# Loading expert weights 1 MB at a time, with neighbouring rows of K in one partition

## What is computed

```python
D_MODEL = 2048; SEQ = 512; N_EXPERTS = 16; TOP_K = 2; D_EXPERT = 512; MOE_BLOCK = 128

def moe_ffn(h, w_router, router_bias, w1, w3, w2):
    ...
    order = jnp.argsort(flat_e)
    ...
    xb = h[buf_tok].reshape(n_blocks, MOE_BLOCK, D)

    def expert_block(args):
        xblk, e = args
        return (jax.nn.silu(xblk @ w1[e]) * (xblk @ w3[e])) @ w2[e]
    ...
    return jnp.zeros_like(h).at[stok].add(yb[dest] * sgate[:, None].astype(h.dtype))
```

## Time and profile before

| what | value |
|---|---|
| time, median of 3 runs | 2569.21 us (2564.76 to 2570.18) |
| profiled execution: its span, first to last instruction | 2558.9 us |
| median less this span | 10.3 us |
| PE busy / VectorE (DVE) / ScalarE (ACT) / GpSimd (POOL) | 89% / 62% / 37% / 24% of the span |
| share of PE in the chain that ended last | 74% |
| DMA | 532 MB, 208 GB/s in the mean; 366 to 392 GB/s in the expert stage |
| granted clock of PE, mean | 0.951 |

### The profile page before, as it was taken

The page is one execution under the profiler, slowest core; times in us unless marked ns, Lnnn a source line. Parts: engine busy times, 40 slices in busy tenths (PEclk is TensorE's granted clock), DMA queues, the critical chain, the costliest instruction groups (busy, mean ns, idle before and its releaser), DMA issues.

```text
span 2558.9 us, 35674 instructions
## 1 busy us (share of the span) xinstructions
PE 2279.9 (89%) x11413; PEld 1875.1 (73%) x11413; DVE 1582.4 (62%) x1942; ACT 947.6 (37%) x1130; POOL 607.5 (24%) x698
## 2 busy tenths in 40 slices
PE   2579999999999999799999998998579999999990
PEld 1179888888888888477777876777557777777770
DVE  2177545555556554566666664523579999999984
ACT  3044322222122212322222222222158777777771
POOL 0035414424443443211111110100201221221222
PEclk9889999999999999799999999999589999999995
DMA  9945422222222222377777775632479999999985
GB/s 375 410 130 164 134 83 77 66 84 68 78 72 76 73 79 74 107 224 226 219 229 234 230 220 198 219 116 70 164 250 368 382 375 390 366 373 392 372 340 214
DMA packets 386604, 532.12 MB, mean 208 GB/s; under 512 B 15072, under 2 KB 261344, under 8 KB 379008
## 3 DMA queue, kind: packets, MB, share of 16 engines
q1 hardware_dynamic: 353216, 392.93, 44.7%
q0 software_dynamic: 33344, 138.63, 15.5%
HBM read 494.77 MB, written 36.73 MB: 208 GB/s over the span
## 4 chain that ended last, share of the span: by engine, by line
PE 74%; DVE 6%; issue 3%; ACT 2%; DMA 2%; POOL 1%; ACTq 0%; SPq 0%; POOLq 0%; DVEq 0%
PE ps L614 11%; PE ps L616 11%; PE ps L615 11%; PE ps L894 6%; PE ps L896 5%; PE ps L895 5%; PE ps L676 4%; DVE e_lo L1776 2%; PE ps L801 2%; PE ps L844 2%; PE ps L802 2%; PE ps L845 2%; PE ps L846 2%; PE ps L803 2%; PE ps L916 1%
## 5 line engine op out<-in xcount | busy, mean ns | idle before, releaser
L1349 DVE TENSOR_TENSOR w_lo<-raw,w_hi 128x1024 fp32r<-128x1024 f32 x272 | 345.0, 1270 | 339.8 <-ACT w_hi L1012 338.6
L1012 ACT CAST w_hi<-raw 128x1024 fp32r<-128x1024 f32 x272 | 285.0, 1049 | 690.4 <-PE ps L616 368.5
L1776 DVE TENSOR_TENSOR e_lo<-e_raw,e_hi 128x1024 fp32r<-128x1024 f32 x384 | 501.8, 1329 | 59.7 <-ACT e_hi L1220 47.8
L614 PE MATMUL ps<-hl_hi,w_hi 128*128 128x512 f32 x1280 | 510.7, 399 | 0.5 <-DVE s_ctx L1422 0.5
L616 PE MATMUL ps<-hl_hi,w_lo 128*128 128x512 f32 x1280 | 499.9, 391 | 0.0
L615 PE MATMUL ps<-hl_lo,w_hi 128*128 128x512 f32 x1280 | 499.1, 390 | 0.0
L1220 ACT CAST e_hi<-e_raw 128x1024 fp32r<-128x1024 f32 x384 | 401.0, 1059 | 162.9 <-PE ps L896 117.5
L616 PEld LDWEIGHTS ps<-hl_hi,w_lo 128*128 128x128 f32 x1280 | 240.8, 188 | 51.6
L614 PEld LDWEIGHTS ps<-hl_hi,w_hi 128*128 128x128 f32 x1280 | 241.2, 188 | 49.3 <-issue 1.7
L615 PEld LDWEIGHTS ps<-hl_lo,w_hi 128*128 128x128 f32 x1280 | 241.3, 189 | 49.1 <-issue 1.7
L894 PE MATMUL ps<-e_hi,xe_hi 128*128 128x512 f32 x512 | 206.6, 404 | 36.1 <-DVE e_lo L1776 33.2
(11 more groups left out here) (331 smaller groups left out, 3681.1 us busy)
## 6 DMA issues: line engine op xcount, KB each, us to landing
e_raw<-in_w_e SPq DMA_DIRECT2D x384, 512.0 KB, 6.9
raw<-in_w_in SPq DMA_DIRECT2D x208, 512.0 KB, 3.7
ada<-in_w_ada POOLq DMA_DIRECT2D x64, 1024.0 KB, 6.0
ada_ring<-in_w_ada SPq DMA_DIRECT2D x16, 2048.0 KB, 17.1
raw<-in_w_out SPq DMA_DIRECT2D x32, 512.0 KB, 4.0
block_outputs<-y_sb POOLq DMA_DIRECT2D x32, 512.0 KB
raw<-in_w_branch_pool SPq DMA_DIRECT2D x16, 512.0 KB, 3.9
raw<-in_w_branch_hgrn SPq DMA_DIRECT2D x16, 512.0 KB, 3.9
```

Source lines behind the costliest of these rows:

```text
L614: mm(dst, hi, rhs_hi[:, k, :], start=(k == 0), stop=False)
L1012: act_e.copy(w_hi[:, hslot, :], raw[:, slot, :]).then_inc(hi_done, 1)
L1349: tt(w_lo[:, hslot, :], raw[:, slot, :], w_hi[:, hslot, :].bitcast(F32), ALU.subtract).then_inc(split_done, 1)
L1776: tt(e_lo[:, hslot, :], e_raw[:, slot, :], e_hi[:, hslot, :].bitcast(F32), ALU.subtract).then_inc(e_split, 1)
```

## The change

The three expert weights are viewed with `(p k)` for `(k p)`: row d = 16 p + k of w_e1 and w_e3 lies in partition p, and row d = 4 p + k of w_e2. A load now takes four neighbouring rows of w_e1 or w_e3, or one whole row of w_e2, for each partition: 2048 numbers, 8 KB in one run, 1 MB in all. It fills two neighbouring slots of `e_raw`; the ring has four such pairs, each with one semaphore. SP waits until both units of the pair that was there are split. There are 12 loads an expert for 24. Casts, splits and matmuls stay at units of 512 KB. So that the tokens agree with the new order of rows, a transpose of `xe` reads every 16th column, one of `act` every 4th.

```diff
--- before.py
+++ after.py
@@ -138,9 +138,9 @@
     w_bh_d = w_branch_hgrn[0].rearrange("(k p) n -> p k n", p=P)
     w_out_d = w_out[0].rearrange("(k p) n -> p k n", p=P)
     w_pg_d = w_pool_group[0].rearrange("g (k p) n -> p g k n", p=P)
-    w_e1_d = w_e1[0].rearrange("e (k p) n -> e p k n", p=P)
-    w_e3_d = w_e3[0].rearrange("e (k p) n -> e p k n", p=P)
-    w_e2_d = w_e2[0].rearrange("e (k p) n -> e p k n", p=P)
+    w_e1_d = w_e1[0].rearrange("e (p k) n -> e p k n", p=P)
+    w_e3_d = w_e3[0].rearrange("e (p k) n -> e p k n", p=P)
+    w_e2_d = w_e2[0].rearrange("e (p k) n -> e p k n", p=P)
     w_r_d = w_router.rearrange("(k p) n -> p k n", p=P)
 
     mod_d = nc.dram_tensor("mod_rows", [1, 4 * D], F32).ap()
@@ -390,7 +390,7 @@
         score_rdy, sel_rdy, pos_mm, onehot_rdy, tab_mm, table_rdy = (sem(s) for s in (
             "score_rdy", "sel_rdy", "pos_mm", "onehot_rdy", "tab_mm", "table_rdy"))
 
-        e_in = raw_in + [sem("e_in6"), sem("e_in7")]
+        e_in = raw_in[0:4]
         e_hi_done, e_split, e_units = sem("e_hi_done"), sem("e_split"), sem("e_units")
         xe_in, xe_T, xe_hi_rdy, xe_rdy = (sem(s) for s in (
             "xe_in", "xe_T", "xe_hi_rdy", "xe_rdy"))
@@ -421,7 +421,7 @@
             return SLOTS + s + 1
 
 
-        E_BASE = [16 * (U_M // SLOTS + KT + 8)] * 4 + [16 * (U_M // SLOTS + KT)] * 2 + [0] * 2
+        E_BASE = 16 * (U_M // SLOTS + KT + 8)
 
 
         @block.sync
@@ -517,35 +517,30 @@
             sp.wait_ge(h2_rdy, NTOK - 1)
             sp.wait_ge(h2_last, 1)
 
-            def load_e(g, slot, src):
-                sp.wait_ge(e_split, g + 1)
+            def load_e(n, slot, src):
+                sp.wait_ge(e_split, n * 2 + 2)
                 sp.sem_inc(sp_own, 1)
-                sp.dma_start(e_raw[:, slot, :].rearrange("p (k n) -> p k n", k=src.shape[1]), src
+                sp.dma_start(e_raw[:, 2 * slot:2 * slot + 2, :].rearrange("p a b -> p (a b)"), src
                              ).then_inc(e_in[slot], 16)
 
-            def w13(w, e, q):
-                return w[ds(e, 1), :, 2 * q:2 * q + 2, :].rearrange("o p k n -> (o p) k n")
-
-            def w2(e, q):
-                return w_e2_d[ds(e, 1), :, q // 2:q // 2 + 1, 1024 * (q % 2):1024 * (q % 2) + 1024
-                              ].rearrange("o p k n -> (o p) k n")
-
-            for q in range(16):
-                load_e(q, q % 8, w13(w_e1_d if q < 8 else w_e3_d, 0, q % 8))
+            def piece(e, n):
+                w, k, rows = (w_e1_d, n, 4) if n < 4 else (w_e3_d, n - 4, 4) if n < 8 else (w_e2_d, n - 8, 1)
+                return w[ds(e, 1), :, rows * k:rows * k + rows, :].rearrange("o p k n -> (o p) (k n)")
+
+            for n in range(8):
+                load_e(n, n % 4, piece(0, n))
             with sp.Fori(1, E) as e:
-                for q in range(24):
-                    src = w13(w_e1_d, e, q) if q < 8 else w13(w_e3_d, e, q - 8) if q < 16 else w2(e - 1, q - 16)
-                    load_e(e * 24 + (q - 8), q % 8, src)
-            for q in range(8):
-                load_e(E * 24 - 8 + q, q, w2(E - 1, q))
+                for n in range(12):
+                    load_e(e * 12 + (n - 4), n % 4, piece(e, n) if n < 8 else piece(e - 1, n))
+            for n in range(8, 12):
+                load_e(E * 12 - 12 + n, n % 4, piece(E - 1, n))
             sp.wait_ge(table_rdy, 1)
             n_extra = sp.value_load(route_i[0:1, 7:8], min_val=0, max_val=NXTRA)
             with sp.Fori(0, NXTRA) as b:
                 with sp.If(b < n_extra):
                     e = sp.value_load(route_i[0:1, ds(b, 1)], min_val=0, max_val=E - 1)
-                    for q in range(24):
-                        src = w13(w_e1_d, e, q) if q < 8 else w13(w_e3_d, e, q - 8) if q < 16 else w2(e, q - 16)
-                        load_e(b * 24 + (E * 24 + q), q % 8, src)
+                    for n in range(12):
+                        load_e(b * 12 + (E * 12 + n), n % 4, piece(e, n))
                 sp.nop()
 
             for i in range(NTOK):
@@ -914,13 +909,14 @@
                 pe.wait_ge(actT_rdy, b + 1)
                 for j in range(4):
                     last = pe.transpose(ps[:, 6 + part % 2, j * P:(j + 1) * P],
-                                        xe[:, (4 * part + j) * P:(4 * part + j + 1) * P], ident[:])
+                                        xe[:].rearrange("t (p k) -> t k p", k=KT)[:, 4 * part + j, :], ident[:])
                 last.then_inc(xe_T, 1)
 
             def turn_act(b):
                 pe.wait_ge(act_rdy, b + 1)
                 for j in range(4):
-                    last = pe.transpose(ps[:, 6, j * P:(j + 1) * P], act[:, j * P:(j + 1) * P], ident[:])
+                    last = pe.transpose(ps[:, 6, j * P:(j + 1) * P],
+                                        act[:].rearrange("t (p k) -> t k p", k=4)[:, j, :], ident[:])
                 last.then_inc(act_T, 1)
 
             def x_ready(b):
@@ -1215,7 +1211,7 @@
 
 
             def e_hi_unit(g, slot, hslot, uses):
-                act_e.wait_ge(e_in[slot], uses + E_BASE[slot])
+                act_e.wait_ge(e_in[slot // 2], uses + E_BASE)
                 act_e.wait_ge(e_units, g + 1)
                 act_e.copy(e_hi[:, hslot, :], e_raw[:, slot, :]).then_inc(e_hi_done, 1)
```

## The result

| | median of the timed runs | ratio to before, 95% interval | span of the profiled execution |
|---|---|---|---|
| before | 2569.69 us (4 runs, 2564.76 to 2571.45) | | 2558.9 us |
| after | 2600.85 us (4 runs, 2592.35 to 2605.99) | 1.0122 [1.0094, 1.015] | 2600.4 us |

The changed kernel is 31 us slower. Two slow executions further down, one of e8_three_pairs (3802.95 us) and one of the kernel before beside it (3406.05 us), are left out of the medians and ratios.

The account below looks back on a forecast made before the run. PE was taken as the bound, the DMA engines nearly one. Span 2558.9 - 1.4 (waits for xe_lo) + 0 (coarseness, small edits) + 0 (transposes) = 2557.5, with timed runs 10.3 us above: 2567.8 us; range 2560 to 2593.

Parts of the forecast that it names:

- the second rival: Expert stage: the coarse ring of 1 MB loads starves ScalarE's casts, 2575 to 2586 us; chance 0.15.
- the price of coarseness: Expert weight loads: later issue and waiting for all of 1 MB cost 0, up to 2.0 us an expert in the range.
- From issue to landing, "5.7 us" for 1 MB: Expert weight loads: 4.5 us where the queue had just run dry, plus 1.24 for 512 KB more.
- so it holds: Quiet part of a turn: a pair lands 5.7 us after issue, ScalarE needs it after about 6.9, no loss.
- Landed at 2114.4 or somewhat later: Tight place: the pair lands 8.7 us after 2105.7; first cast 0.9 us late, inside PE's 1.25 us of cover.
- Nine of the fourteen experts: Experts without half clock have no spare room; each loses 0.75 us (2575 us) or 2.0 us (2586 us).
- Faster runs: Expert weight loads: runs of 8 KB move 422 GB/s, over 415 when saturated, giving the engines 2.2 us of room per expert.
- What of it reaches the end, 1.4 us at most: Only PE's waits for xe_lo made by DMA can be gained: 1.4 us in the whole run.
- The transposes at 0: Strided weight loads of xe and act stay hidden under the identity's pass, starts 0.11 us apart: cost 0.
- The first rival: Strided weight loads of transposes outrun the identity's pass: 22.4 us slower, 2590.2 us; chance 0.27.
- PE's old waits stay: PE's waits behind act's transposes, 0.31 and 2.06 us an expert, come from POOL's multiply and remain.
- The places at half clock: Expert stage: five stretches partly at 1.2 GHz cost 1.5 us each; missing all five gives 2560 us; chance 0.10.

Follow-up runs that it names:

- e8_three_pairs: The changed kernel with three pairs of slots for four: 2669.70 us, ratio 1.0399 to the kernel before.
- e2: The kernel before with the new order of rows and strided transposes, still 512 KB loads in eight slots, runs of 4 KB: 2573.05 us, ratio 1.0018.
- e9: The kernel before with twelve slots of 512 KB for eight: 2565.02 us, ratio 1.0007.
- e1: The kernel before with the strided transposes alone: 2570.57 us, ratio 1.0009.
- e10: The kernel before without POOL's multiply of y_sb in the stage, the product made once for each token at the end: 2549.47 us, ratio 0.9935.
- e5: The kernel before, 512 KB loads, but a load for an even slot waits until its neighbour is split too: 2581.55 us, ratio 1.0076.
- e3: The kernel before, old order of rows and plain transposes, but loads of 1 MB in four pairs of slots: 2607.0 us, ratio 1.0158.
- e4: The changed kernel with the plain transposes of before: 2593.65 us, ratio 1.0103 to the kernel before.
- e6: The changed kernel with six pairs of slots for four: 2568.56 us, ratio 1.0031 to the kernel before.
- e12: The changed kernel with six pairs of slots and POOL's multiply taken out of the stage: 2533.66 us, ratio 0.9869 to the kernel before.
- e13: New order of rows, 512 KB loads in runs of 4 KB, twelve slots, POOL's multiply taken out of the stage: 2535.12 us, ratio 0.9876.

## Why the prediction was wrong

It was wrong: the result lies above the range, and the mechanism was the second rival's, which had a chance of 0.15. Even that rival's dear end, 2586 us, is 15 us short.

**The step that failed: the price of coarseness, taken as 0.** Its terms, beside what the trace of the changed kernel has:

1. *From issue to landing, "5.7 us" for 1 MB.* That was 4.5 us, the shortest landing of 512 KB, plus 1.24 for the bytes. Measured were 7.3 us in the median, and at the tight place these (the view of L523, 2117 to 2126 us):

```profile
L523 SPq DMA_DIRECT2D e_raw<-in_w_e x3: 333/333/333, 2117.9 to 2125.6; - x3
...
DMA to landing us min/median/max: 8.6/8.6/10.4
```

   The prediction took the least of the landings where their median stood in the same row, and the median of the page beside it.
2. *"In the quiet part of a turn ScalarE needs the pair about 6.9 us after the issue", "so it holds".* There the landings are these (2219 to 2243 us):

```profile
DMA to landing us min/median/max: 6.9/7.1/8.3
```

   A margin of 1.2 us was counted; in fact there is none. So the ring runs at its limit here too and, as it seems, enters the tight place with nothing in reserve. The sum in item 3 started from a ring in order.
3. *"Landed at 2114.4 or somewhat later", 14.4 us behind the end of the first slow e_lo.* In the changed kernel the corresponding loads of one expert were issued at 2117.88, 2122.71 and 2125.57 and landed at 2126.43, 2131.30 and 2135.94; the last is 18.1 us behind, so that cast was 3.7 us later than forecast. Of these, 2.9 are the first load, 8.55 us from issue to landing where 5.7 were taken. The other 0.8 are the 3.67 MB behind it: 9.5 us for 8.7, 386 GB/s for 422. The first load's way can be seen in the trace. SP had issued nothing from 2112.85 to 2117.88, and the 16 engines were at a share of 0.59 just before, where before had them full (windows as above; the first is of the kernel before, at the same place ahead of its 2100.0):

```profile
2097.00:2100.00 3.00, 2.70 (x14) 2.02 (x13) 1.66 (x2) 3.00 (x4) 2.33 (x2) 1.00 1.06 388
```

```profile
2117.00:2120.00 3.00, 2.17 (x11) 1.37 (x9) 3.00 (x2) 2.79 (x5) 2.67 (x2) 1.00 0.59 171
```

   The single packets show the rest. In the microsecond before the new load begins to move, at 2120.51, SP's queue carries 27 GB/s, one packet at a time, all that is left of the load before; and the new load then shares the engines with POOL's stores. With 0.9 us late against 1.25 of cover by the forecast, 3.3 us were left; PE waited 2.35 of them in two pieces.
4. *"Nine of the fourteen experts", up to 2.0 us each.* The rival supposed that an expert with a stretch at half clock has room to spare. The waits came in all: 1.47 us in the mean at the three units, and 0.8 more for what follows (xe_lo, small gaps, half clock, transposes): 2.3 us times 15. By nine experts at 2.0 us the rival's dear end was 2586 us; by fifteen at 2.3 us it would have been about 2602.

In one sentence: the price of coarseness was taken as 0 because a 1 MB load was given the least landing seen (4.5 us) plus its bytes, 5.7 us, where it takes 7.3 in the median and 8.6 at the tight place. Rows of before would have warned: the margin of 1.2 us in item 2 is smaller than the scatter of the landings that it rests on (4.5 to 7.7 us).

The Trainium skill, "DMA: Bandwidth & Descriptors", section Bandwidth, advises transfers of at least 1 MiB for three quarters of the peak. Here 512 KB in eight slots already moved 371 to 386 GB/s over an expert, more than three quarters of the 431 of the first stage, and 1 MB in four pairs 352 to 358: in a ring of fixed room the number of loads under way decided. With half as much room again, and POOL's multiply gone, 1 MB moved 415 and 512 KB in runs of 4 KB 411.

**The steps that held.**
- *Faster runs.* Forecast over 415 GB/s in the saturated part, measured 423. *What of it reaches the end, 1.4 us at most:* the medians of e2 and e9 show no gain, and e9's trace the 2.7 us of waits for xe_lo (by the starts of matmuls) that there were to gain.
- *The transposes at 0.* The load grew by what the prediction allowed it to grow unseen, and the starts stayed close: (0.61 - 0.27) / 3 = 0.113 us, against 0.11. e1 puts the whole at 0.09% [-0.11, 0.29]. The first rival (0.27) falls. In the account above they are 0.16 us an expert, 2.4 us in all, below what the medians can tell. The rows of the changed kernel:

```profile
L911 PEld LDWEIGHTS ps<-ident,xe 128*128 128x128 f32 x192 | 28.1, 194 | 12.8 <-DVE xe_lo L1777 10.1
L918 PEld LDWEIGHTS ps<-ident,act 128*128 128x128 f32 x48 | 7.6, 204 | 0.9
```

  The Trainium skill, "Advanced Engine Details and Errata", section SBUF Cachelines, asks for two hits on a line of 16 B. The loads agree: 54 and 65 ns more than the 140 and 139 of before, where the 128 columns took about 55. What decided was that this stayed under the cover.
- *PE's old waits stay.* 0.27 and 2.05 us. Their cause, argued from rows before, is shown by e10: no e_lo is over 1.23 us there, for up to 3.80 before. The Trainium skill, "SBUF — State Buffer", section SBUF: two separate sides, names such a port pair, which a VectorE instruction with two operands in SBUF and one of GpSimd that reads SBUF take in turns. The trace agrees: 3.80 us is about one multiply (2.4) and one e_lo (1.22) in a row, and e10 has no such unit.
- *The places at half clock* (0.10) moved little: 0.61 to 0.72 us an expert.
- *The sign from the second rival's own test.* PE waits for e_lo at the seventh unit, behind casts released by a landing, as written.

**What stays open.** Why packets get longer with few loads under way (below), and why the end of a load can trail by 3 us. How the loss divides between late release and late landing, beyond e5 and e3. The 12 us of scatter ahead of the stage, and with it whether the 0.31% of six pairs are real.

## What to carry to other kernels

Coarser transfers in a ring of fixed room buy rate with depth: count how many loads are under way at the tightest place, and time them from issue to landing by the median of rows at such a place, with what other queues move beside them, not by the shortest. If the margin is smaller than the scatter of those landings, it is no margin. A ring that is just deep enough shows nothing (twelve slots brought nothing before), so look for the bound that hides it; with POOL's multiply gone and the ring half as deep again, the same 1 MB loads were part of one of the two fastest kernels here.

## What was not expected of the hardware

These figures are from the single packets in the traces; a packet is one run of a load.

- **A load takes 7 us even where its bytes need 2.5.** One 1 MB load in the quiet part was issued at 2221.05 us. By counting 128 packets for each load in order, its first byte moved at 2223.25 and its last at 2226.62, and it landed at 2228.18: 2.2 us, 3.4 us, 1.6 us. It was not alone: 14 to 17 packets of SP's loads were moving at any time from 2222.5 to 2229.9, and the landings around it came 2.44 to 3.5 us apart (2224.72, 2228.18, 2230.62, 2233.08). Where more loads were queued they came 2.47 us apart (2138.40, 2140.88, 2143.35). The time from issue to landing and the distance of landings are two things; a shallow ring pays for the first.
- **A load can trail.** The load issued at 2112.85 moved most of its bytes by 2117.3; its last packets went one at a time, 0.31 us each, until 2120.18, and it landed at 2120.53. That looks like a single DMA engine behind the others, but the trace doesn't name engines.
- **Packets get longer with few loads under way.** An 8 KB packet takes 309 ns in the median; single ones took up to 2479 in the changed kernel. Counted by how many SP loads were between issue and landing when it started (1960 to 2440 us), the share of packets over one and a half times the median is, in the changed kernel, 8.5% with one, 10.2% with two, 2.1% with three and 0.0% with four; with six pairs it is 8.8, 8.2, 0.8 and 0.0%. Over the stage that makes 6.4% in the changed kernel, 6.1% in e4, 9.3% in e8, 3.4% in e6, 3.7% in e3 (runs of 2 KB for w_e1 and w_e3). Loads of 512 KB have fewer: 0.7% before, 1.3% in e2, 1.4% in e5, 1.1% in e9. Why was not found.
- **Rate by length of run,** one engine's bytes over the median packet: 2 KB in 84 ns (e3; 86 before), 4 KB in 159, 8 KB in 309, 16 KB in 611; that is 24.4, 25.8, 26.5 and 26.8 bytes a ns. From 4 to 8 KB it is 3%, which fits that e12 and e13 come out alike.
